# Six local re-orderings in a two-block transformer kernel: lead-in, softmax ends, feed-forward start, retention, recurrence, last norm

## The chip, the core and the metric

The kernel runs on one core of a Trainium2 chip. The metric is the device time of one execution in microseconds (us); the table further down gives the median of three runs. The engines run side by side and meet at semaphores: TensorE (PE) does the matrix products, VectorE (DVE) and ScalarE (ACT) the work on elements, GpSimd (POOL) a few additions, and SyncE (SP) issues the DMAs that bring the weights.

## The reference

Two blocks follow each other on a sequence of 256 rows of 1024 values. The first has two layers of three parallel attention branches and a gated feed-forward part with a convolution; the second has four layers (retention, a linear recurrence, latent attention, retention), each with a feed-forward part. Cut to what matters here:

```python
def first_block(x, ...):  # x: 1 x 256 x 1024, two layers
    for i in range(DEPTH):
        h = rms_norm(x, attn_norm[i])
        qa, ka, va, qb, kb, vb, qc, kc, vc, gates = jnp.split(h @ w_in[i], SPLIT_POINTS, axis=-1)
        ya = moba_attention(...)  # per head: rms_norm, rope, softmax(q k^T) v
        yb = sliding_window_sink_attention(...)
        yc = differential_attention(...)
        g = jax.nn.sigmoid(gates.reshape(B, S, N_BRANCH, D))
        merged = g[:, :, 0] * (ya @ w_pa[i]) + g[:, :, 1] * (yb @ w_pb[i]) + g[:, :, 2] * (yc @ w_pc[i])
        x = x + merged @ w_out[i]
        h = rms_norm(x, mlp_norm[i])
        u = causal_depthwise_conv(h @ w_up[i], conv_w[i], conv_b[i])   # 3 taps
        gate_u, val_u = jnp.split(u, 2, axis=-1)   # 2816 columns each
        x = x + (jax.nn.silu(gate_u) * val_u) @ w_down[i]
    return x

def second_block(x, ...):  # four layers: retention, rg-lru, mla, retention
    for i in range(DEPTH_2):
        mix = (retention_mixer, rglru_mixer, mla_mixer)[i % 3](h, ...)
        h = layer_norm(ALPHA * h + mix, ln_g[i, 0], ln_b[i, 0])
        h = layer_norm(ALPHA * h + square(relu(h @ w1[i])) @ w2[i], ln_g[i, 1], ln_b[i, 1])
    return h
```

All of it is computed in float32 from weights in HBM, some 375 MB in all, that are read once.

## The kernel before

**Tiling.** The sequence stands in two tiles of 128 rows (`tt` is 0 or 1). Each weight matrix is read in slots of 1 MB (128 x 2048 float32) into a ring of five buffers (`raw`, in the trace `slot`). To keep float32 accuracy, each slot is parted in a high and a low half: ACT copies it rounded to `slot_hi` (line 1460), DVE subtracts that from the slot into `slot_lo` (line 1955). The activations are parted in the same way (`split` tiles). A product is the sum of three: high x high, low weights x high, high weights x low, so a slot against both row tiles is 24 matmuls of 128 x 512 on PE.

**Rings and waits.** `slots` hands out the five buffers; SP waits for `slot_free` before it loads one. `banks` hands out the eight PSUM banks of 128 x 512 (`bank`; the upper four are also the accumulator `acc`); `banks.use(n, ...)` says how many are in use from there on and where the round starts. PE waits for `bank_read` before it fills a bank, the reading engine for `bank_full`. Each engine runs its own program in its own order, written out by hand; nothing passes an instruction that waits. `weights.ahead(u)` emits the splits of the slots up to three behind `u`, `weights.through(u)` those up to `u` itself.

**The stretches that the change touches.** Each engine has its own function of the same name.

- *Start.* ACT issues the two halves of `x`, SP the identity matrix, the gain table `tab`, and the slots of `w_in`. `rms_norm` squares (ACT 1495), takes the root (ACT 1497), scales (DVE 2012); PE turns the rows (`turned`, line 728) and ACT and DVE write the high and low parts (`hi_rows`, `lo_rows`). `head` on PE runs the first row tile over the first two slots, then the second. Behind the sixth slot SP issues twelve small loads `tokc` (line 592), and behind those the seventh slot.
- *Softmax ends.* `divisors(g)` on DVE (line 2186) scales the five groups of probabilities by their sums; PE turns them.
- *Feed-forward of the first block.* Eleven steps `s`, each with two slots of `w_up` (`gv` 0 is the gate half, 1 the value half). The products of step 0 come out of the head as rows and are turned back by PE (`turned_back`), and DVE copies them (line 2350); in the other steps each half has two sums `j` of one bank, which `summed(s, gv, j)` (line 2328) adds up. ACT scales (`scaled`), `convolved(s, gv)` on DVE (line 2338, four instructions) adds the other taps, ACT applies silu, POOL multiplies (line 2809), and ACT and DVE part the result (`hi_hidden`, `lo_hidden`). In layer 0 `angles(s - 1)` on DVE (lines 2060 to 2083) also computes, one piece a step, the rotation angles for the second block.
- *Retention.* Behind the four heads of group norm, `low(0)` to `low(7)` (line 2537) write the low parts of the turned gated rows; PE's next turning waits for the banks that `low` reads.
- *Recurrence.* `scans` (line 2642) run the recurrence on tiles of 128 channels, `gated` (2648) multiplies by the gate, `high_rows` on ACT (1828) and `low_rows` on DVE (2653) part the result. The groups are those of `LRU_ROWS`: 2, 4 and 4 tiles. `project("lwo", 5)` multiplies it by the five slots of `w_o`, slot c taking the tiles of channels in order.
- *End.* The last `layer_norm(7, True)` follows the last matmul: sum (DVE 2387), mean, squares (ACT 1698), root (ACT 1700), reciprocal, scale (DVE 2392, 2398), and four stores by SP.

## Time and profile before

| | us |
|---|---|
| median of 3 runs | 2083.84 |
| lowest, highest | 2083.83, 2084.2 |
| the profiled execution | 2085.47 |
| its span | 2083.7 |
| PE busy | 2050.8 (98%) |
| DVE busy | 1528.6 (73%) |
| ACT busy | 1052.6 (51%) |
| POOL busy | 158.7 (8%) |
| mean DMA rate | 181 GB/s |

The profiled execution took 1.63 us more than the median run, and 1.77 us of its time lie outside the span. Times in the rows count from the start of the span. A matmul's end is modelled, so neighbouring PE rows overlap a little; a stop of PE is best read from start to start, which makes it some 0.15 us longer than the idle time that the views give (at 1238.09 PE was idle for 1.45, but the matmul before started at 1236.25, and its kind follow each other by 0.23: 1.61). The granted clock (PEclk) is TensorE's clock in the stretch as a share of full speed: 1.00 stands for 2.4 GHz and 0.50 for 1.2 GHz.

### The profile page before, as it was taken

What the parts mean: (1) busy time and instruction counts of PE and PEld (TensorE: products, weight loads), DVE (VectorE), ACT (ScalarE), POOL (GpSimd) and SP (SyncE); (2) the same over time, 40 slices, a digit from 0 to 9 for tenths busy, and PEclk for the clock granted to TensorE, in tenths of its full rate; (3) what the DMA queues carried; (4) which work ended last, traced back from release to release, by engine and by line L of the source; (5) the groups of instructions that cost most, each with busy time, mean ns of one, the idle gap of its engine ahead of it and who ended that gap; (6) DMA issues with size and microseconds to landing.
All of it is one profiled execution on the core that took longest, in us unless ns stands there. A gap on an engine that the chain in (4) does not pass through costs nothing.

```text
span 2083.7 us, 27288 instructions
## 1 busy us (share of the span) xinstructions
PE 2050.8 (98%) x11335; PEld 1768.6 (85%) x11335; DVE 1528.6 (73%) x1677; ACT 1052.6 (51%) x1232; POOL 158.7 (8%) x94
## 2 busy tenths in 40 slices
PE   7999999999999999999999999999999999999998
PEld 6998888899978888878888988888888888778887
DVE  5878799787979777665766797666876667566665
ACT  4564555556556545454534575344653445455432
POOL 2001011030101204100000000000000005000000
PEclk9999999999999999999999999999999999999999
DMA  7544555564445555545655646654456556455662
GB/s 257 173 141 158 166 197 197 166 216 139 148 158 198 184 188 189 182 167 173 214 196 182 207 155 200 211 188 144 159 184 218 185 183 209 148 182 182 206 197 101
DMA packets 244724, 377.68 MB, mean 181 GB/s; under 512 B 14085, under 2 KB 179194, under 8 KB 244602
## 3 DMA queue, kind: packets, MB, share of 16 engines
q1 hardware_dynamic: 244314, 374.90, 54.6%
q8 instruction: 90, 1.47, 0.3%
q10 hardware_dynamic: 288, 1.05, 0.1%
q14 instruction: 32, 0.26, 0.0%
HBM read 374.87 MB, written 1.05 MB: 180 GB/s over the span
## 4 chain that ended last, share of the span: by engine, by line
PE 87%; DVE 6%; ACT 2%; DVEq 2%; DMA 1%; issue 0%; SPq 0%; ACTq 0%
PE bank L730 44%; PE acc L730 41%; DVE slot_lo L1955 3%; DVEq L1950 2%; PE bank L728 2%; ACT slot_hi L1460 1%; DMA slot<-in_w_in 1%; PE acc L728 0%; DVE arena L2029 0%; DVE arena L2186 0%; DVE arena L2642 0%; SPq L592 0%; DVE arena L2299 0%; DVE arena L2338 0%; ACT arena L1455 0%
## 5 line engine op out<-in xcount | busy, mean ns | idle before, releaser
L1955 DVE TENSOR_TENSOR slot_lo<-slot,slot_hi 128x2048 fp32r<-128x2048 f32 (+1 forms) x344 | 794.1, 2315 | 285.6 <-ACT slot_hi L1460 284.7
L1460 ACT ACTIVATE slot_hi<-slot 128x2048 fp32r<-128x2048 f32 (+1 forms) x344 | 652.1, 1904 | 386.7 <-DMA slot<-in_mlp_w 313.0
L730 PE MATMUL acc<-slot_hi,split 128*128 128x512 f32 (+1 forms) x2236 | 703.3, 389 | 2.9 <-DVE split L2653 1.5
L730 PE MATMUL bank<-split,slot_hi 128*128 128x512 f32 (+1 forms) x2524 | 575.3, 357 | 7.2 <-DVE arena L2328 6.9
L730 PEld LDWEIGHTS bank<-split,slot_hi 128*128 128x128 f32 x2524 | 439.6, 190 | 66.6 <-issue 8.6
L730 PEld LDWEIGHTS acc<-slot_hi,split 128*128 128x128 f32 x2236 | 418.1, 188 | 88.4 <-DVE split L2282 1.9
L730 PE MATMUL acc<-slot_lo,split 128*128 128x512 f32 (+1 forms) x1118 | 432.7, 387 | 0.0
L730 PE MATMUL bank<-split,slot_lo 128*128 128x256 f32 x2094 | 354.7, 283 | 0.0
L730 PEld LDWEIGHTS bank<-split,slot_lo 128*128 128x128 f32 x2094 | 310.7, 191 | 16.5
L730 PEld LDWEIGHTS acc<-slot_lo,split 128*128 128x128 f32 x1118 | 210.4, 188 | 39.7 <-issue 1.0
L730 PE MATMUL bank<-slot_hi,split 128*128 128x512 f32 (+1 forms) x804 | 227.7, 391 | 3.4 <-ACT split L1478 2.6
L730 PEld LDWEIGHTS bank<-slot_hi,split 128*128 128x128 f32 x804 | 150.3, 190 | 34.3 <-issue 4.6
L730 PE MATMUL bank<-slot_lo,split 128*128 128x512 f32 (+1 forms) x402 | 132.4, 388 | 0.0
L730 PE MATMUL acc<-split,slot_hi 128*128 128x256 f32 (+1 forms) x668 | 130.5, 305 | 0.0
L730 PEld LDWEIGHTS acc<-split,slot_hi 128*128 128x128 f32 x668 | 107.3, 191 | 5.7 <-issue 1.3
L1658 ACT ACTIVATE arena<-arena,par 128x256 f32<-128x256 f32 x88 | 48.1, 594 | 124.7 <-DVE arena L2328 117.6
L2411 DVE TENSOR_REDUCE arena<-bank 128x256 f32<-128x512 f32 x112 | 76.1, 687 | 42.9 <-PE bank L730 42.9
L1455 ACT ACTIVATE arena<-bank 128x512 f32<-128x512 f32 (+2 forms) x104 | 56.9, 569 | 91.2 <-PE bank L730 87.8
L2827 POOL TENSOR_TENSOR arena<-arena 128x512 f32<-128x512 f32 x16 | 28.0, 1753 | 955.7 <-ACT arena L1455 955.7
L730 PE MATMUL acc<-split,slot_lo 128*128 128x256 f32 x398 | 94.2, 283 | 0.0
L730 PEld LDWEIGHTS bank<-slot_lo,split 128*128 128x128 f32 x402 | 76.0, 189 | 16.0 <-issue 0.5
L2338 DVE SCALAR_TENSOR_TENSOR arena<-arena,par 128x254 f32<-128x254 f32 (+1 forms) x176 | 76.9, 479 | 3.6 <-issue 0.4
(230 smaller groups left out, 1476.0 us busy)
## 6 DMA issues: line engine op xcount, KB each, us to landing
slot<-in_mlp_w SPq DMA_DIRECT2D x128, 1024.0 KB, 5.3
slot<-in_ret_w_in SPq DMA_DIRECT2D x48, 1024.0 KB, 5.2
slot<-in_w_up SPq DMA_DIRECT2D x40, 1024.0 KB, 5.1
slot<-in_w_in SPq DMA_DIRECT2D x38, 1024.0 KB, 5.3
slot<-in_w_down SPq DMA_DIRECT2D x22, 1024.0 KB, 4.9
slot<-in_ret_w_o SPq DMA_DIRECT2D x16, 1024.0 KB, 4.8
slot<-in_lru_w_in SPq DMA_DIRECT2D x10, 1024.0 KB, 5.3
slot<-in_w_out SPq DMA_DIRECT2D x8, 1024.0 KB, 4.8
```

Of the source, the lines that this page charges most:

```text
L728: i = nc.tensor.transpose(o, w, ident)
L730: i = nc.tensor.matmul(o, w, m, start=start, stop=stop)
L1455: return A(o, i, func, **kw).then_inc(bank_read[u.r], 1)
L1460: A(whi[u.r][:, 0:u.cols], raw[u.r][:, 0:u.cols], ACT.Copy).then_inc(slot_hi[u.r], 1)
L1658: i = A(cgv[:, 2 * (s % 2) + j, gv, :], up_sums(s, gv, j), ACT.Identity, scale=par[:, L, PF_CW + 4 * FFT + f:PF_CW + 4 * FFT + f + 1], bia ...
L1950: dve.drain()
L1955: TTO(wlo[u.r][:, 0:u.cols], raw[u.r][:, 0:u.cols], f32(whi[u.r][:, 0:u.cols]), ALU.subtract)\
L2338: i = STT(out=y, in0=up_sums(s, gv, j)[:, 0:S - sh], scalar=par[:, L, PF_CW + (2 - sh) * 2 * FFT + f:PF_CW + (2 - sh) * 2 * FFT + f + 1], ...
L2411: RED(hq[:, s % NHID, j, :], bank[u.r][:, :].rearrange("p (i s) -> p s i", i=2), AX, ALU.add)\
L2827: TTO(rin[c % 2], rsum[c % 2][:, :, 0:S], rsum[c % 2][:, :, S:2 * S], ALU.add).then_inc(V["rot_summed"], 1)
```

## The change

Nothing of what is computed changes, and no load or split of weights is added or left out, except that the first slot's come in halves.

1. *Start.* `x[1]` is loaded by SP behind the first slot instead of by ACT at once. The first slot is loaded by two DMAs of 512 KB with a semaphore of their own for the first, and its high and low parts are made by halves (`first_norm` on ACT and DVE). The large `consts` load goes behind the fourth slot instead of the second. PE does twelve turnings of the identity into an unused bank before the first real one, and `first_head` runs both row tiles over the first slot, then both over the second. The projections that follow start at bank 4.
2. *Softmax ends.* `divisors(4)` stands ahead of the split of the first `w_p` slot.
3. *Feed-forward start.* ACT copies step 0's banks instead of DVE, scales step 0 at once, and its splits stand between; DVE's first three steps are written out with each `summed` ahead of a convolution. In the later steps ACT's `hi_hidden` goes from behind `scaled(s, 0)` to behind the next split, ahead of `scaled(s, 1)`. In layer 0 the angles start at step 3 (`angles(s - 3)`), and steps 9 and 10 take two pieces.
4. *Retention.* `low(0)` and `low(1)` stand in the step of the last head, ahead of a split.
5. *Recurrence.* The last four tiles go in two groups of two, with `gated(3)`, `high_rows(3)` and `low_rows(3)`.
6. *Last norm.* For the second row tile the last matmuls end by column halves, DVE takes mean and variance from `bn_stats` and `bn_aggr`, and ACT does the root alone.

```diff
-LRU_ROWS = (slice(0, 2), slice(2, 6), slice(6, 10))
+LRU_ROWS = (slice(0, 2), slice(2, 6), slice(6, 8), slice(8, 10))
...
-banks.use(NBANK)
+banks.use(NBANK, None, NSUM)
...
+if L == 0 and i == 0:
+    u = slots[f"w_in{L}", c]
+    sp.wait_ge(slot_free[u.r], u.uses + 1)
+    dst, src = what[0](u.r)
+    sp.dma_start(dst[:, 0:2, :], src[:, 0:2, :]).then_inc(V["first_loaded"], 16)
+    sp.dma_start(dst[:, 2:4, :], src[:, 2:4, :]).then_inc(slot_full[u.r], 16)
+    sp.dma_start(x[:, 1, :], I["x"][0, P:2 * P, :]).then_inc(V["x_loaded1"], 16)
+    continue
 put(slots[f"w_in{L}", c], *what)
-if i == 1 and L == 0:
+if i == 3 and L == 0:
     sp.dma_start(con[:, P:C_ALL], I["consts"][:, P:C_ALL]).then_inc(V["loaded"], 16)
 if i == 12:
...
+def first_rows_high(u, o, name):
+    w = [part[u.r][:, :].rearrange("p (k n) -> p k n", n=512) for part in (whi, wlo)]
+    h = hT[0][:, 0:4, 0:P]
+    pe.wait_ge(V["hi_out"], his[name, (0, 0)].uses + 1)
+    for a, halves in enumerate(((V["first_hi"], slot_hi[u.r]), (V["first_lo"], slot_lo[u.r]))):
+        for b in range(2):
+            pe.wait_ge(halves[b], 1)
+            for k in (2 * b, 2 * b + 1):
+                mm(o[:, :], h[:, k, :], w[a][:, k, :], (a, k) == (0, 0), False)
...
+def first_head(name, turned, us, bs):
+    for _ in range(12):
+        mm(bank[NBANK - 1][:, 0:P], ident, None, transpose=True)
+    turned(0)
+    opened = [open_bank(bs[0])]
+    first_rows_high(us[0], opened[0][0], name)
+    rows_low(us[0], opened[0][0], name, 0, 0, None)
+    turned(1)
+    opened.append(open_bank(bs[1]))
+    rows_high(us[0], opened[1][0], name, 1, 0)
+    rows_low(us[0], opened[1][0], name, 1, 0, None)
+    freed(us[0])
+    for tt in range(TT):
+        rows_high(us[1], opened[tt][0], name, tt, 1)
+        rows_low(us[1], opened[tt][0], name, tt, 1, opened[tt][1])
+    freed(us[1])
...
+    acc_halves(u, lhs[i], tt)
+    continue
 acc_rows(u, lhs[i], tt, False, last, V["acc_full"] if last else slot_free[u.r] if tt else None,
...
-project("lwo", 5, lru_rows, lambda c: pe.wait_ge(V["lru_y"], (1, 2, 2, 3, 3)[c]), ln_turned(2))
+project("lwo", 5, lru_rows, lambda c: pe.wait_ge(V["lru_y"], (1, 2, 2, 3, 4)[c]), ln_turned(2))
...
+squared(0)
+rooted(0)
+act.wait_ge(V["first_loaded"], 16)
+A(whi[r][:, 0:SLOT // 2], raw[r][:, 0:SLOT // 2], ACT.Copy).then_inc(V["first_hi"], 1)
+hi_rows(name, 0, [0])
+act.wait_ge(slot_full[r], 16)
+A(whi[r][:, SLOT // 2:SLOT], raw[r][:, SLOT // 2:SLOT], ACT.Copy).then_inc(slot_hi[r], 1)
+weights.next = 1
+squared(1)
+hi_rows(name, 0, [1])
+rooted(1)
+hi_rows(name, 1)
...
+back_copies(f"uph{L}", [0])
+weights.ahead(slots[f"up{L}", (0, 0)])
+back_copies(f"uph{L}", [1], 1)
+weights.ahead(slots[f"up{L}", (0, 1)])
+for gv in range(2):
+    u = banks[f"up{L}", (0, gv)]
+    full(act, u)
+    copy(cu[:, gv, :], bank[u.r][:, :], u)
...
-for s in range(11):
+for gv in range(2):
+    scaled(0, gv)
+weights.ahead(slots[f"up{L}", (1, 0)])
+silu(0, L * 11)
+for s in range(1, 11):
     n = L * 11 + s
     for gv in range(2):
         weights.ahead(slots[f"up{L}", (s, gv)])
+        if gv:
+            hi_hidden(s - 1, n - 1)
         scaled(s, gv)
-        if s and gv == 0:
-            hi_hidden(s - 1, n - 1)
     silu(s, n)
...
 high_rows(2)
+high_rows(3)
...
+def first_norm(name):
+    r = slots.made[0].r
+    scaled_rows(0, 0)
+    for c0, hi, lo in ((0, V["first_hi"], V["first_lo"]), (SLOT // 2, slot_hi[r], slot_lo[r])):
+        c = slice(c0, c0 + SLOT // 2)
+        dve.wait_ge(hi, 1)
+        TTO(wlo[r][:, c], raw[r][:, c], f32(whi[r][:, c]), ALU.subtract).then_inc(lo, 1)
+    weights.next = 1
+    lo_rows(name, 0, [0])
+    scaled_rows(0, 1)
+    lo_rows(name, 0, [1])
+    lo_rows(name, 1, [0])
+    weights.upto(1)
+    lo_rows(name, 1, [1])
...
 scores(4)
 divisors(3)
 y_low(2)
+divisors(4)
 weights.through(slots[f"w_p{L}", 0])
-divisors(4)
 weights.through(slots[f"w_p{L}", 1])
...
 summed(1, 0, 0)
-for gv in range(2):
-    u = banks[f"up{L}", (0, gv)]
-    full(dve, u)
-    T(cu[:, gv, :], bank[u.r][:, :]).then_inc(bank_read[u.r], 1)
 weights.ahead(slots[f"up{L}", (0, 1)])
-for gv in range(2):
-    convolved(0, gv)
-for s in range(1, 11):
+summed(1, 0, 1)
+convolved(0, 0)
+summed(1, 1, 0)
+convolved(0, 1)
+weights.ahead(slots[f"up{L}", (1, 0)])
+summed(1, 1, 1)
+summed(2, 0, 0)
+weights.ahead(slots[f"up{L}", (1, 1)])
+summed(2, 0, 1)
+convolved(1, 0)
+lo_hidden(his[f"hidb{L}", 0], 0)
+summed(2, 1, 0)
+convolved(1, 1)
+weights.ahead(slots[f"up{L}", (2, 0)])
+summed(2, 1, 1)
+weights.ahead(slots[f"up{L}", (2, 1)])
+for s in range(2, 11):
     for gv in range(2):
-        for j in range(2):
-            if (s, gv, j) != (1, 0, 0):
+        if s > 2:
+            for j in range(2):
                 summed(s, gv, j)
-        weights.ahead(slots[f"up{L}", (s, gv)])
+            weights.ahead(slots[f"up{L}", (s, gv)])
         convolved(s, gv)
         if gv == 0:
             lo_hidden(his[f"hidb{L}", s - 1], (s - 1) % NHID)
     if s > 2:
         weights.ahead(slots[f"down{L}", s - 2])
-    if L == 0:
-        angles(s - 1)
+    if L == 0 and s > 2:
+        angles(s - 3)
+        if s > 8:
+            angles(s - 1)
...
+def last_rows(n):
+    cs = [slice(h * 512, (h + 1) * 512) for h in range(HALVES)]
+    for h, c in enumerate(cs):
+        dve.wait_ge(V["acc_full"], 8 + 2 * n + 2 + h)
+        STT(out=xn[:, 1, c], in0=x[:, 1, c], scalar=ALPHA, in1=acc[:, 1, c], op0=ALU.mult, op1=ALU.add)
+        d()
+        nc.vector.bn_stats(col(BN + 6 * h, 6), xn[:, 1, c])
+    d()
+    nc.vector.bn_aggr(col(MV, 2), col(BN, 12))
+    d()
+    TS(col(LVAR), col(MV + 1), LN_EPS, None, ALU.add).then_inc(V["ln_mean"], 1)
+    for h, c in enumerate(cs):
+        STT(out=x[:, 1, c], in0=xn[:, 1, c], scalar=col(MV), in1=tab[:, c], op0=ALU.subtract, op1=ALU.mult)
+        if h == 0:
+            dve.wait_ge(V["ln_std"], 2 * n + 2)
+            nc.vector.reciprocal(col(LR + 1), col(LSTD + 1))
+        d()
+        STT(out=x[:, 1, c], in0=x[:, 1, c], scalar=col(LR + 1), in1=tab[:, D + h * 512:D + (h + 1) * 512],
+            op0=ALU.mult, op1=ALU.add).then_inc(V["out_ready"], 1)
...
     for tt, u in enumerate(us):
         TS(ro[:, tt, h * RDV:(h + 1) * RDV], bank[u.r][:, :], col(MV + 2 * tt), col(LR + tt),
            ALU.subtract, ALU.mult).then_inc(bank_read[u.r], 1)
+    if h == 3:
+        for i in range(2):
+            low(i)
     weights.ahead(slots[k + "w", 17 + 2 * h])
     if h:
         gated(h - 1)
-for i in range(2):
-    low(i)
 gated(3)
...
-scans(range(6, 10))
-for c in (8, 9):
-    evacuated(dve, banks["lw", c])
+scans((6, 7))
+evacuated(dve, banks["lw", 8])
 gated(2)
+scans((8, 9))
+low_rows(2)
 weights.ahead(slots["lwo", 0])
-low_rows(2)
+evacuated(dve, banks["lw", 9])
+gated(3)
+low_rows(3)
...
```

**The start on ACT.** The rows behind the first root, before: the whole first slot (`slot_49`), both halves of the first turned rows, the second slot, then the squares of `x[1]`.

```order
L1460 ACTIVATE slot_hi<-slot_49 128x2048 [waits slot_full0]
L1478 ACTIVATE split<-bank 128x4x128 [waits bank_full0]
L1478 ACTIVATE split<-bank 128x4x128 [waits bank_full1]
L1460 ACTIVATE slot_hi<-slot_50 128x2048 [waits slot_full1]
L1495 ACTIVATE xn,stat<-x 128x1024 [waits x_loaded1]
L1497 ACTIVATE stat<-stat 128x1 [waits var_ready]
L1478 ACTIVATE split<-bank 128x4x128 [waits bank_full3]
```

And now:

```order
L1559 ACTIVATE slot_hi<-slot_49 128x1024 [waits first_loaded]
L1524 ACTIVATE split<-bank 128x4x128 [waits bank_full0]
L1562 ACTIVATE slot_hi<-slot_49 128x1024 [waits slot_full0]
L1549 ACTIVATE xn,stat<-x 128x1024 [waits x_loaded1]
L1524 ACTIVATE split<-bank 128x4x128 [waits bank_full1]
L1553 ACTIVATE stat<-stat 128x1 [waits var_ready]
L1524 ACTIVATE split<-bank 128x4x128 [waits bank_full3]
L1524 ACTIVATE split<-bank 128x4x128 [waits bank_full0]
L1507 ACTIVATE slot_hi<-slot_50 128x2048 [waits slot_full1]
```

The second slot's copy moved behind all four `hi_rows`, and the squares of `x[1]` now stand between the two first ones.

**The feed-forward start on DVE**, layer 0, from `summed(1, 0, 0)` on, before (`slot_50` to `slot_53` and `slot_49` are the ring's buffers; 2328 is `summed`, 2350 the copy of step 0, 2338 `convolved`):

```order
L2328 TENSOR_REDUCE arena<-bank 128x256 [waits bank_full0]
L2350 COPY arena<-bank 128x512 [waits bank_full3]
L2350 COPY arena<-bank 128x512 [waits bank_full2]
L1955 TENSOR_TENSOR slot_lo<-slot_52,slot_hi 128x2048 [waits slot_hi3]
L2338 SCALAR_TENSOR_TENSOR arena<-arena,par 128x255 [waits conv_scaled]
L2338 SCALAR_TENSOR_TENSOR arena<-arena,par 128x255
L2338 SCALAR_TENSOR_TENSOR arena<-arena,par 128x254 x2
L2338 SCALAR_TENSOR_TENSOR arena<-arena,par 128x255 [waits conv_scaled]
L2338 SCALAR_TENSOR_TENSOR arena<-arena,par 128x255
L2338 SCALAR_TENSOR_TENSOR arena<-arena,par 128x254 x2
L2328 TENSOR_REDUCE arena<-bank 128x256 [waits bank_full1]
```

And now (2426 is `summed`, 2436 `convolved`):

```order
L2426 TENSOR_REDUCE arena<-bank 128x256 [waits bank_full0]
L2036 TENSOR_TENSOR slot_lo<-slot_52,slot_hi 128x2048 [waits slot_hi3]
L2426 TENSOR_REDUCE arena<-bank 128x256 [waits bank_full1]
L2436 SCALAR_TENSOR_TENSOR arena<-arena,par 128x255 [waits conv_scaled]
L2436 SCALAR_TENSOR_TENSOR arena<-arena,par 128x255
L2436 SCALAR_TENSOR_TENSOR arena<-arena,par 128x254 x2
L2426 TENSOR_REDUCE arena<-bank 128x256 [waits bank_full3]
L2436 SCALAR_TENSOR_TENSOR arena<-arena,par 128x255 [waits conv_scaled]
```

`summed(1, 0, 1)`, the row on `bank_full1`, stood behind two copies, a split and eight convolution rows; now one split stands between it and the sum ahead of it.

**The end of the recurrence on DVE**, before (`slot_50` holds the fourth slot of `w_o`, `slot_51` the fifth):

```order
L1955 TENSOR_TENSOR slot_lo<-slot_49,slot_hi 128x2048 [waits slot_hi0]
L2642 SCALAR_TENSOR_TENSOR arena<-arena 128x256 x4
L2648 TENSOR_TENSOR arena<-arena 128x1024 [waits bank_read3,bank_read2]
L1955 TENSOR_TENSOR slot_lo<-slot_50,slot_hi 128x2048 [waits slot_hi1]
L2653 TENSOR_TENSOR split<-arena,split 128x1024 [waits hi_out]
L1955 TENSOR_TENSOR slot_lo<-slot_51,slot_hi 128x2048 [waits slot_hi2]
L1955 TENSOR_TENSOR slot_lo<-slot_52,slot_hi 128x2048 [waits slot_hi3]
```

And now:

```order
L2036 TENSOR_TENSOR slot_lo<-slot_49,slot_hi 128x2048 [waits slot_hi0]
L2776 SCALAR_TENSOR_TENSOR arena<-arena 128x256 x2
L2782 TENSOR_TENSOR arena<-arena 128x512 [waits bank_read2]
L2776 SCALAR_TENSOR_TENSOR arena<-arena 128x256 x2
L2787 TENSOR_TENSOR split<-arena,split 128x512 [waits hi_out]
L2036 TENSOR_TENSOR slot_lo<-slot_50,slot_hi 128x2048 [waits slot_hi1]
L2782 TENSOR_TENSOR arena<-arena 128x512 [waits bank_read3]
L2787 TENSOR_TENSOR split<-arena,split 128x512 [waits hi_out]
L2036 TENSOR_TENSOR slot_lo<-slot_51,slot_hi 128x2048 [waits slot_hi2]
L2036 TENSOR_TENSOR slot_lo<-slot_52,slot_hi 128x2048 [waits slot_hi3]
```

The scans, the gating and the low part went from one row group to two, and the second group's two rows stand between the two last splits of the projection.

**The same place on ACT**, before (1828 is `high_rows`) and now (1908 is `high_rows`):

```order
L1828 ACTIVATE split<-arena 128x1024 [waits lru_product]
L1460 ACTIVATE slot_hi<-slot_49 128x2048 [waits slot_full0]
L1460 ACTIVATE slot_hi<-slot_50 128x2048 [waits slot_full1]
L1828 ACTIVATE split<-arena 128x1024 [waits lru_product]
L1460 ACTIVATE slot_hi<-slot_51 128x2048 [waits slot_full2]
L1460 ACTIVATE slot_hi<-slot_52 128x2048 [waits slot_full3]
```

```order
L1908 ACTIVATE split<-arena 128x1024 [waits lru_product]
L1507 ACTIVATE slot_hi<-slot_49 128x2048 [waits slot_full0]
L1507 ACTIVATE slot_hi<-slot_50 128x2048 [waits slot_full1]
L1908 ACTIVATE split<-arena 128x512 [waits lru_product] x2
L1507 ACTIVATE slot_hi<-slot_51 128x2048 [waits slot_full2]
L1507 ACTIVATE slot_hi<-slot_52 128x2048 [waits slot_full3]
```

The copy of `slot_51` stood behind one `high_rows`; now it stands behind two.

## Rows read from the trace of the kernel before

**Rows 1.** Who PE waited for, whole run: idle us, times, longest.

```profile
PE bank L730 <- DVE arena L2328: 6.9, 2, 3.4
PE bank L728 <- DVEq L2540: 1.5, 4, 0.4
```

**Rows 2.** Timeline, PE at the start: start, us, instruction, count, [idle before <-releaser].

```profile
13.16 2.04 PE L730 MATMUL bank<-slot_hi,split 128*128 128x512 f32 x4 [2.57 <-ACT split L1478]
...
24.02 1.98 PE L730 MATMUL bank<-slot_hi,split 128*128 128x512 f32 x8
...
28.59 0.47 PE L730 MATMUL bank<-slot_hi,split 128*128 128x512 f32 x1 [0.79 <-issue]
```

**Rows 3.** Timeline, ACT at the start.

```profile
10.62 1.91 ACT L1460 ACTIVATE slot_hi<-slot 128x2048 fp32r<-128x2048 f32 x1 [4.46 <-DMA slot<-in_w_in]
```

**Rows 4.** Timeline, DVE at the start.

```profile
7.56 0.16 DVE L2008 RECIPROCAL stat<-stat 128x1 f32<-128x1 f32 x1 [1.64 <-DMA tab<-in_attn_norm]
```

**Rows 5.** Busy by stretch: PE, PEld, DVE, ACT, POOL, PEclk, DMA share, GB/s.

```profile
235.18:240.44 5.26, 5.26 (x17) 4.49 (x17) 5.18 (x7) 3.36 (x4) 0.65 (x1) 0.50 0.59 199
...
615.68:620.06 4.38, 4.38 (x16) 3.66 (x17) 4.30 (x5) 3.37 (x4) 0.66 (x1) 0.61 0.62 201
...
13.00:18.20 5.20, 5.04 (x12) 3.78 (x13) 5.20 (x5) 3.33 (x5) 0.00 (x0) 1.00 1.04 390
```

**Rows 6.** DMA issues by line: count, KB each, median us to landing.

```profile
slot<-in_w_up SPq DMA_DIRECT2D x40, 1024.0 KB, 5.1
...
slot<-in_w_up SPq DMA_DIRECT2D x8, 512.0 KB, 4.9
```

**Rows 7.** The chain that ended last, 0 to 95 us: start, us, what.

```profile
25.34 0.38 SPq L523
...
31.54 11.90 DMA slot<-in_w_in
```

**Rows 8.** Timeline, PE at four later stops.

```profile
85.01 1.09 PE L728 MATMUL bank<-con,arena 128*128 128x128 f32 x8 [0.47 <-DVE arena L2143]
...
157.37 0.87 PE L728 MATMUL bank<-con,arena 128*128 128x128 f32 x6 [0.57 <-DVE arena L2186]
...
195.81 0.50 PE L730 MATMUL acc<-slot_hi,split 128*128 128x512 f32 x1 [0.51 <-DVE split L2282]
...
1238.09 0.50 PE L730 MATMUL acc<-slot_hi,split 128*128 128x512 f32 x1 [1.45 <-DVE split L2653]
```

**Rows 9.** Timeline, DVE in the first feed-forward steps.

```profile
230.87 3.56 DVE L2338 SCALAR_TENSOR_TENSOR arena<-arena,par 128x255 f32<-128x255 f32 x8
```

**Rows 10.** Timeline, DVE with the angles and at the feed-forward's end, layer 0.

```profile
350.38 2.13 DVE L2076 SCALAR_TENSOR_TENSOR arena<-trig,arena 128x1024 f32<-128x1024 f32 x1
...
370.94 0.69 DVE L2328 TENSOR_REDUCE arena<-bank 128x256 f32<-128x512 f32 x1 [2.00 <-PE bank L730]
...
385.79 0.69 DVE L2050 TENSOR_TENSOR split<-arena,split 128x512 fp32r<-128x512 f32 x1 [0.70 <-ACT split L1671]
```

**Rows 11.** POOL's product of the feed-forward, whole run: ns min/median/max.

```profile
L2809 POOL TENSOR_TENSOR arena<-arena x20: 1268/3218/3228, 234.6 to 744.5; 128x512 f32<-128x512 f32 x20
```

**Rows 12.** Timeline, a split on DVE beside POOL's additions.

```profile
174.15 3.42 DVE L1955 TENSOR_TENSOR slot_lo<-slot,slot_hi 128x2048 fp32r<-128x2048 f32 x1
```

**Rows 13.** Timeline, DVE in the retention, then at the recurrence's end.

```profile
923.91 2.29 DVE L1955 TENSOR_TENSOR slot_lo<-slot,slot_hi 128x2048 fp32r<-128x2048 f32 x1 [1.49 <-ACT slot_hi L1460]
...
1234.62 2.28 DVE L1955 TENSOR_TENSOR slot_lo<-slot,slot_hi 128x2048 fp32r<-128x2048 f32 x1
1236.82 1.22 DVE L2653 TENSOR_TENSOR split<-arena,split 128x1024 fp32r<-128x1024 f32 x1
1237.95 4.49 DVE L1955 TENSOR_TENSOR slot_lo<-slot,slot_hi 128x2048 fp32r<-128x2048 f32 x2
```

**Rows 14.** Timeline, ACT at the recurrence's end.

```profile
1235.70 5.76 ACT L1460 ACTIVATE slot_hi<-slot 128x2048 fp32r<-128x2048 f32 x3
```

**Rows 15.** Timeline, DVE at the end.

```profile
2076.04 1.22 DVE L2387 SCALAR_TENSOR_TENSOR xn<-x,acc 128x1024 f32<-128x1024 f32 x1 [3.29 <-PE acc L730]
```

102 lines of the change are left out of this document (57 added, 45 removed).

## The prediction

> **What bounds the kernel now.** I read the shares of busy time first: TensorE is busy for 98% of the span, so only its stops can be won, and the stretch in which its clock is low. The second view is the list of waits of PE. Of it two lines matter: 6.9 us in two stops behind `summed` and 1.5 us in four stops behind `low` [rows 1]. The timeline of PE gives the single stops: the first matmul of a weight at 13.16, one short stop at 28.59 [rows 2], then 85.01, 157.37, 195.81 and 1238.09 [rows 8]. For each stop I went to the engine named at its end and read what stands ahead of the awaited instruction there; where that chain is back to back, taking one link out of PE's own wait wins nothing. Last I read the stretches with their granted clock, since a stop can cost more than itself: behind the first feed-forward stop the clock is at 0.50 for 5.26 us, in layer 1 at 0.61 for 4.38 us, where it is near 1 elsewhere [rows 5].
>
> **1. Start.** The first slot is ready for PE 13.16 because it landed at about 10.6 and its high part took 1.91 more [rows 2, 3]. The DMA share is 1.04 there, at 390 GB/s [rows 5], so bytes decide. `x`, identity, gain table and first slot are about 2.6 MB, landed by 10.6. Counting back at 0.37 MB a us (my estimate between that row's 0.39 and the somewhat lower rate of the beginning): without `x[1]` ahead of it the table lands near 6.2 instead of 7.5 [rows 4], half the slot at 7.7, the other at 9.1, `x[1]` at 10.6. First half's high part to 8.7, first matmul near 9.5, 3.6 earlier. This lead isn't kept whole. `x[1]`'s squares, its scaling and the `hi_rows` put its turned rows on ACT until about 16.6, and only behind them stands the high part of the second slot, 18.5, and DVE's low part, 20.8. PE has done both tiles of the first slot at about 18.9, starts the second, stands for about 1 us for the low part, and has 20 matmuls of 0.227 us (eight take 1.98, the last 0.39 of it being pipeline [rows 2]) left: 25.4 where it is 27.65 now (sixteen from 24.02 on), 2.3 earlier. The stop at 28.59 (0.9 from start to start) came from a bank that now is another one, and goes: 3.2. At 85.01 a stop of 0.6 waits for DVE [rows 8]. That chain begins with the seventh slot, issued at 31.54, 6.2 behind the sixth at 25.34, and landing 11.9 later [rows 7]. The sixth slot's buffer now is free at about 18.9, the seventh's at 25.4, so it can be issued 6.1 earlier; if it only lands earlier by as much as the bytes ahead of it, the gain is 3.2. PE could gain 3.2 + 0.6. I take **-3.4**, bounds -2 and -5.
>
> The rows show two loads of 512 KB landing in 4.9 us where 1024 KB take 5.1 [rows 6]: on a queue with room, halving a load wins almost nothing. The Trainium skill ("DMA: Bandwidth & Descriptors", Anatomy of one DMA and Rules for kernel authors) goes the same way against this part: about 2.0 us fixed for each DMA plus bytes at 436 GB/s, at least 1 MiB for each, and spreading over issuing engines gives no bandwidth. By it half a slot alone would take an estimated 3.2 us and the whole 4.4, so the halving would win 1.2, and the move of `x[1]` to another queue only its place behind the slot; the start's gain would be some -2.5 instead of -3.4, and the sum 0.9 later.
>
> **2. Softmax ends.** The stops at 157.37 and 195.81 are 0.7 each. The first waits for `divisors(4)`, behind a split; that goes. The second waits for a low part at the end of a row of splits, sums and low parts on DVE that has hardly a gap from 161 on. The moved split is done no earlier than now, since `divisors(4)` itself waits for exponentials till nearly that time, so the row begins no earlier and what is won at the first stop is added at the second. **0** for both layers, bounds -1.5 (both stops of both layers half gone) and +0.4.
>
> **3. Feed-forward start, layer 0.** The stop is 3.4 idle [rows 1], 3.6 from start to start; the 5.26 us at clock 0.50 lose 2.6 [rows 5]. `summed(1, 0, 1)` stood behind eight convolution rows of 3.56 us [rows 9], two copies and a split that waited for ACT; it now stands behind one split. The order on DVE has slack of some 2.8 us to PE's demand by my count, ACT's copies are needed later than they are done, so both parts go: -6.2. Then the angles. Moving them back by two steps puts one more piece of 2.13 us [rows 10] into step 9 and one into step 10. At step 9 DVE idles 2.0 before 370.94 [rows 10] and hides it. In step 10 DVE has no gap: the last hidden low part, at 385.79 to 386.5 [rows 10], comes 2.2 to 2.5 later, at about 388.8, where PE asks for it near 387.3: a stop of 1.6; the rest of the lag goes on to the next norm, 0.5. Together +2.1. **-4.1**, bounds -6.2 (the tail is hidden) and -3.
>
> **4. Feed-forward start, layer 1.** No angles. 3.6 and 39% of 4.38, 1.7 [rows 1, 5]: **-5.3**, bounds -5.5 and -3.6 (the clock falls for another reason).
>
> **5. Retention.** Two stops a time, 1.5 idle in four, 0.15 more each from start to start: 2.1. `low(0)` and `low(1)`, 1.9 us together, go to where DVE has just been idle for 1.49 [rows 13], so nothing late follows but 0.4. **-2.1**, bounds -2.1 and -1.
>
> **6. Recurrence.** PE stops 1.6 at 1238.09 [rows 8]. Fourth slot's low part: from 1234.62, done at 1236.9 [rows 13]; the last low rows of all four tiles at 1238.0. By pairs, the first pair's rows are ready ahead of that split, so the fourth slot's product starts at 1237.0: 1.1 earlier. But the fifth slot's high part, on ACT, now stands behind `high_rows(3)`, which waits for `gated(3)`, which on DVE stands behind the split of the fourth slot: 1236.9 + 0.65 = 1237.6, `high_rows(3)` to 1238.2, the high part (5.76 / 3 = 1.92 [rows 14]) to 1240.1, DVE's low part (4.49 / 2 = 2.24 [rows 13]) to 1242.4. Now it is done at 1240.2, and PE wants it at 1238.09 + 12 x 0.227 = 1240.8. So **+1.6**, and PE stands for 2.7 in one piece (1239.7 to 1242.4). The trace has no stop of that length in this place: one of 1.45 is not followed by a low clock, two of 3.4 are [rows 1, 5, 8]. 2.7 is nearer to 3.4, so I add 1.6, about the smaller of the two losses (1.7): **+3.2**, bounds -1.6 (the stop just goes) and +4.2.
>
> **7. Last norm.** From 2076.04 DVE adds, means, scales till 2081.2 [rows 15]. By halves the first half's sum and statistics lie beside the last six matmuls; behind the last one stand one sum of 0.7, one `bn_stats` of 0.65, the aggregate 0.25 and four waits on DVE's own results, where 1.22, a mean and 1.15 of squares on ACT stood. The first store leaves 0.7 earlier, the second hardly. **-0.2**, bounds -1 and +0.2.
>
> Sum: -3.4 + 0 - 4.1 - 5.3 - 2.1 + 3.2 - 0.2 = -11.9. On the profiled execution's 2085.5 that is 2073.6, with its 1.6 above the median taken off **2071.9**.
>
> **Rivals.** *(a) No low clock behind the recurrence's stop*, as behind 1.45: 2070.3. For it: the stop is short of 3.4. *(b) The orders pay as meant*: the softmax stops go for good (-1.5) and the fifth slot is in time because the scans of a pair are done earlier than I count (-1.1 instead of +3.2): 2071.9 - 1.5 - 4.3 = 2066.1. Against it is the row order on ACT. *(c) The start gives -2 and the retention -1*, DVE's chain to 85 being bound by landings: 2074.4. *(d) The feed-forward starts only shift their stop*, because ACT, with four copies more ahead of its scaling, is late for the first `convolved`: half of 11.5 stays, 2077.6. *(e) Slower*: in the feed-forward of layer 0 DVE becomes the bound of every step. Its step is four sums of 0.65, three splits of 2.24, 3.56 of convolution and a low part of 0.65, 13.5 us [rows 9, 10, 13], 15.6 with angles, beside PE's three slots or 72 x 0.227 = 16.4. POOL's product takes 3.22 us in most steps where 1.27 is its lowest [rows 11], and a split beside POOL's additions took 3.42 instead of 2.28 [rows 12]; if the new order lets the product lie beside three splits, DVE's step is 15.6 + 3 x 1.14 = 19.0, 2.6 over PE's, times 8 steps is 21, of which the tail's 2.1 is part: 2090.8. It decides from 0.8 us more a step on; only half of a step's splits can meet one product, which speaks against it.
>
> **How the numbers follow.** Forecast 0.42, (a) 0.22, (b) 0.15, (c) 0.15, (d) 0.03, (e) 0.03. The likeliest time is 2071.9. From 2065.5, (b) and its bound, to 2075.5, (c) and its bound, lie all but (d), (e) and tails of the unknown prices: 0.8 or a little more. A measurement of this kernel tells about 0.2%, 4.2 us, from no change; below 2079.7 is faster. That holds for all but (e) and part of (d): faster 0.95, the same 0.02, slower 0.03.
>
> **What would show it.** Right: first matmul near 9.5, PE at the place of 28.59 about 3 us earlier; no stop at the second and third feed-forward steps and clock 1 there in both layers; a new stop of about 1.6 at the tail of layer 0's feed-forward behind `lo_hidden`, none in layer 1; the stop of 157 gone and that of 195.8 larger; no stops behind `low`; at the recurrence two stops, the second of 2 to 3 us behind the fifth slot's low part, and a clock below 1 behind it. Wrong: DVE without a gap through layer 0's steps; the start gaining less than 2 at 85; a fifth slot copied by ACT before 1240.

## The result, and the profile after

The changed kernel takes 2069.5 us (median of four runs, 2068.26 to 2070.33) where the kernel before takes 2083.84: 14.3 us or 0.7% less, ratio 0.9927 with a 95% interval of 0.9915 to 0.9939. Timed again on another chip it gave 0.9927 once more (0.9915 to 0.9939). The forecast was 2071.9 with a range of 2065.5 to 2075.5. The profiled execution took 2070.33 us with a span of 2067.7, 16.0 less than the span before; the medians differ by 1.7 less. Half of that is time outside the span, 2.6 us now and 1.8 before, and half is that the profiled execution of before lay 1.6 above its median and this one 0.8.

The waits of PE, changed kernel (who waited for whom, total, times, longest), answer [rows 1]. `summed` (2426 now) and `low` are gone from it, and the longest wait behind a split is the new one in the recurrence; the first row is the wait for the identity before the twelve turnings:

```profile
PE acc L736 <- DMA con<-in_consts: 4.1, 1, 4.1
PE acc L738 <- DVE slot_lo L2036: 3.0, 2, 2.6
PE acc L738 <- DVE split L2380: 0.8, 2, 0.4
```

PE's timeline at the start answers [rows 2]. The first weights are multiplied from 9.73 instead of 13.16, PE stands for the second slot's low part at 20.20, and the stop at 28.59 has no counterpart: `acc` banks are filled from 24.90 on, without one.

```profile
9.73 2.12 PE L738 MATMUL bank<-slot_hi,split 128*128 128x512 f32 x4 [0.21 <-ACT split L1524]
...
20.20 1.21 PE L738 MATMUL bank<-slot_lo,split 128*128 128x512 f32 x4 [0.66 <-DVE slot_lo L2036]
...
24.90 0.39 PE L738 MATMUL acc<-slot_hi,split 128*128 128x512 f32 x1
```

The later stops that are left, from PE's timeline, answer [rows 8]: the one behind the softmax (it has a like one in layer 1, at 565.10), a new one at the tail of layer 0's feed-forward, and two at the recurrence.

```profile
190.55 0.50 PE L738 MATMUL acc<-slot_hi,split 128*128 128x512 f32 x1 [0.41 <-DVE split L2380]
...
376.44 0.50 PE L738 MATMUL acc<-slot_hi,split 128*128 128x512 f32 x1 [0.45 <-DVE split L2146]
...
1219.50 0.47 PE L738 MATMUL acc<-slot_hi,split 128*128 128x512 f32 x1 [0.47 <-DVE slot_lo L2036]
...
1225.08 0.77 PE L738 MATMUL acc<-slot_hi,split 128*128 128x512 f32 x1 [2.58 <-DVE slot_lo L2036]
```

The stretches with their clock (columns as in [rows 5]): the feed-forward's first steps now run at 1.00 in both layers, where [rows 5] have 0.50 and 0.61, and the stretch behind the recurrence's long stop has 0.67.

```profile
1225.08:1230.20 5.12, 5.12 (x16) 4.14 (x17) 4.70 (x3) 2.61 (x3) 0.00 (x0) 0.67 0.01 3
226.29:231.50 5.21, 5.21 (x31) 4.54 (x30) 4.85 (x4) 2.57 (x4) 3.19 (x1) 1.00 0.59 201
600.88:606.00 5.12, 5.12 (x31) 4.45 (x30) 4.77 (x4) 2.58 (x4) 3.19 (x1) 1.00 0.63 205
```

Both programs issue the same matmuls behind the head, so each can be laid beside itself. The lead is how much earlier the changed kernel starts the same matmul; where it changes, a part has its price (a minus sign is a loss):

| place (time before) | lead, us | the part's gain | forecast |
|---|---|---|---|
| head's end, 28.59 | 3.7 | | 3.2 |
| 85.01 | 4.4 | start 4.4 | 3.4 |
| behind 195.81 | 5.3 | softmax, layer 0: 0.9 | 0 |
| 242 | 11.4 | first steps, layer 0: 6.1 | 6.2 |
| 400 | 10.4 | its tail: -1.0 | -2.1 |
| behind 576.35 | 11.2 | softmax, layer 1: 0.8 | 0 |
| 625 | 16.4 | first steps, layer 1: 5.2 | 5.3 |
| behind 929.59 | 17.5 | retention 1.1 | 1.05 |
| 1238.09, fourth slot | 18.6 | 1.1 | 1.1 |
| 1240.99, fifth slot | 15.9 | -2.7 | -2.7 |
| 1245 | 14.2 | clock: -1.7 | -1.6 |
| behind 1850.52 | 15.4 | retention and small shifts 1.2 | 1.05 |
| last store landed | 16.0 | norm and small shifts 0.6 | 0.2 |

### The profile page after: what moved, and what is told of

It is laid out like the page before. It is cut to its first block, busy times and chain, and to the rows that moved or that the text cites. A ratio compares the mean times of both kernels' runs of the same rounds, so it can differ in the third digit from the quotient of the medians.

```text
span 2067.7 us, 27322 instructions
## 1 busy us (share of the span) xinstructions
PE 2049.2 (99%) x11347; PEld 1768.4 (86%) x11347; DVE 1525.6 (74%) x1680; ACT 1052.9 (51%) x1236; POOL 168.1 (8%) x94
## 3 DMA queue, kind: packets, MB, share of 16 engines
HBM read 374.87 MB, written 1.05 MB: 182 GB/s over the span
## 4 chain that ended last, share of the span: by engine, by line
PE 94%; DVE 3%; ACT 1%; DVEq 1%; DMA 0%; issue 0%; SPq 0%
PE bank L738 48%; PE acc L738 44%; PE bank L736 2%; DVE slot_lo L2036 1%; DVEq L2031 1%; ACT slot_hi L1507 1%; PE acc L736 0%; DMA slot<-in_w_in 0%; DVE arena L2776 0%; DVE arena L2782 0%; DVE arena L2397 0%; ACT split L1524 0%; DVE arena L2350 0%; DVE arena L2436 0%; ACT arena L1502 0%
## 5 line engine op out<-in xcount | busy, mean ns | idle before, releaser
L738 PE MATMUL acc<-slot_hi,split 128*128 128x512 f32 x2236 | 713.1, 392 | 4.7 <-DVE slot_lo L2036 3.0
L738 PE MATMUL acc<-slot_lo,split 128*128 128x512 f32 x1118 | 436.7, 391 | 0.0
L738 PE MATMUL bank<-slot_hi,split 128*128 128x512 f32 (+1 forms) x804 | 219.0, 381 | 0.6 <-ACT split L1524 0.6
L2964 POOL TENSOR_TENSOR arena<-arena 128x512 f32<-128x512 f32 x16 | 27.9, 1745 | 958.1 <-ACT arena L1502 958.1
L2946 POOL TENSOR_TENSOR arena<-arena 128x512 f32<-128x512 f32 x20 | 60.6, 3028 | 298.0 <-DVE arena L2436 298.0
```

Of the source, the lines that this page charges most:

```text
L738: i = nc.tensor.matmul(o, w, m, start=start, stop=stop)
L2946: TTO(hq[:, s % NHID, :, :], sgl[:, 2 * (s % 2):2 * (s % 2) + 2, :], cgv[:, 2 * (s % 2):2 * (s % 2) + 2, 1, :], ALU.mult).then_inc(V["prod ...
L2964: TTO(rin[c % 2], rsum[c % 2][:, :, 0:S], rsum[c % 2][:, :, S:2 * S], ALU.add).then_inc(V["rot_summed"], 1)
```

## Experiments

All are the changed kernel with one thing different, and are compared with it by the places at which PE stops and by their leads; a single time scatters by more than most parts are worth. On the chip of the first four, before took 2084.34 us, on that of the next four 2084.89, on the last 2085.32.

**The recurrence in one group.** The edit takes part 5 of the change back, cut to its core:

```diff
-LRU_ROWS = (slice(0, 2), slice(2, 6), slice(6, 8), slice(8, 10))
+LRU_ROWS = (slice(0, 2), slice(2, 6), slice(6, 10))
...
 high_rows(2)
-high_rows(3)
```

> The changed kernel with the recurrence's last four tiles in one group again, all else as changed. Theory: the pairs cost 3.2 us in all (1.0 won at the fourth slot, 2.7 lost at the fifth, 1.6 by the clock at 0.67 of the stretch behind it), so this is about 3 us faster than the changed kernel: 2066.3, one stop of 1.6 near 1219.5, none at the fifth slot, clock 1.00 behind it. Rival: the fifth slot was late for a cause outside this part (its landing, say), so that the stop of 2.7 stays and the fourth slot's grows by 1: 2070.5.

2066.73 us. PE stops once:

```profile
1220.45 0.50 PE L738 MATMUL acc<-slot_hi,split 128*128 128x512 f32 x1 [1.46 <-DVE split L2786]
```

It is 0.95 later than the changed kernel at the fourth slot and 3.4 ahead behind the fifth. The pairs cost what the forecast said, and the rival is out.

**The fifth slot's parts first.**

```diff
 high_rows(2)
+weights.ahead(slots["lwo", 1])
 high_rows(3)
...
 gated(3)
+weights.ahead(slots["lwo", 1])
 low_rows(3)
```

> The changed kernel, with ACT's high part of the fifth slot of w_o ahead of high_rows(3), and DVE's low part of it ahead of low_rows(3). Theory: the fifth slot waited only for its place on ACT; DVE now works without a gap (split of slot 4 to 1219.35, gated(3) to 1220.0, split of slot 5 to 1222.3, low_rows(3) to 1222.95), stops of 0.6 at both slots, the clock stays at 1.00: 2.1 + 1.6 = 3.7 faster than the changed kernel, 2065.8, and 0.5 faster than with one group. Rival: the buffer or the landing of slot 5 is the limit: the stop of 2.7 stays, 2069.5.

2066.29 us. DVE's timeline, and PE's two stops:

```profile
1219.40 0.69 DVE L2783 TENSOR_TENSOR arena<-arena 128x512 f32<-128x512 f32 x1
1220.01 2.28 DVE L2037 TENSOR_TENSOR slot_lo<-slot,slot_hi 128x2048 fp32r<-128x2048 f32 x1
1222.21 0.69 DVE L2788 TENSOR_TENSOR split<-arena,split 128x512 fp32r<-128x512 f32 x1
```

```profile
1219.45 0.47 PE L738 MATMUL acc<-slot_hi,split 128*128 128x512 f32 x1 [0.48 <-DVE slot_lo L2037]
...
1222.95 0.50 PE L738 MATMUL acc<-slot_hi,split 128*128 128x512 f32 x1 [0.51 <-DVE split L2788]
```

DVE runs without a gap and the fifth slot is multiplied from 1222.95, the time worked out. So the place of the fifth slot's two parts was the whole of the long stop; ACT's copy and DVE's split were moved together, and no run moves one alone. What is left, two stops of 0.6, is DVE's own work. Over one group the pairs in this order win 0.2 us at this place of the trace, not 0.5: less than the executions of one kernel scatter. (The trace with one group has one more stop that the others lack, 0.7 at 1455; it isn't part of this.)

**The start as before.** The hunks on the loads, on `first_head`, on both `first_norm` and on `banks.use` taken back.

> The changed kernel with the whole start as before (both x loads by ACT, whole first slot, old head, consts behind the second slot, banks from 0). Theory: the start is worth the lead of 4.4 us that the traces show at the stop of 85.0, and nothing behind depends on it: 2073.9, first matmul of a weight at 13.2, and the softmax gains of 0.8 a layer stay. Rival: the softmax gain of layer 0 came from the earlier DMAs of the start: then 5.2 are lost, 2074.7, and the stop of 0.7 at the fifth divisors is back in layer 0.

2074.58 us, and the stop of before is back:

```profile
84.79 0.87 PE L728 MATMUL bank<-con,arena 128*128 128x128 f32 x6 [0.69 <-DVE arena L2198]
```

4.2 us are lost at that place, and both new divisors' places stay free of a stop: the rival is out. In layer 1 the second stop behind the softmax is 0.4 longer than in the changed kernel (0.78 idle at 569.74), so the two parts are nearly, not quite, independent.

**The angle pieces early.**

```diff
-if L == 0 and s > 2:
-    angles(s - 3)
-    if s > 8:
-        angles(s - 1)
+if L == 0:
+    for a in {3: (0, 1), 4: (2, 3), 5: (4,)}.get(s, (s - 1,) if s > 5 else ()):
+        angles(a)
```

> The changed kernel with the angle pieces 0 to 4 put in steps 3 to 5 and pieces 5 to 9 in steps 6 to 10, one a step as before the change. Theory: the stop of 0.6 at the tail of layer 0's feed-forward comes from piece 7 (1.23 us) in step 10; with it gone the kernel is 0.6 to 0.9 faster than the changed one, 2068.8. Rival: DVE has no room in steps 3 to 5 either and the lag appears there: a stop at step 4 or 5 of 1 to 2 us, 2070.5.

2067.5 us. The tail's stop is gone, and no other stop came. The lead over the changed kernel, 0.3 us from the start, is 1.3 behind the tail: the pieces' place was worth 1.0.

**The softmax order back.**

```diff
-divisors(4)
 weights.through(slots[f"w_p{L}", 0])
+divisors(4)
```

> The changed kernel with divisors(4) behind the split of the first w_p slot again in both layers. Theory (from the two traces): the order itself is worth 0.7 a layer, since the stop behind it did not grow: 1.5 us slower than the changed kernel, stops of 0.7 near 152 and 523. Rival, the forecast's: DVE's row to the next stop is what counts; the new stops are there, but those near 190 and 565 shrink from 0.6 by as much: no difference.

2071.46 us. The stops are there, and those behind them, start to start, have grown from 0.57 to 0.67 and from 0.58 to 0.70 instead of shrinking:

```profile
152.90 0.76 PE L736 MATMUL acc<-con,arena 128*128 128x128 f32 x5 [0.71 <-DVE arena L2284]
...
191.34 0.50 PE L738 MATMUL acc<-slot_hi,split 128*128 128x512 f32 x1 [0.51 <-DVE split L2380]
```

1.7 us are lost from start to start, 0.9 in layer 0 and 0.8 in layer 1. The forecast's zero is wrong, and DVE's timeline shows why. The split behind the merged heads starts at 156.85 here and at 156.82 in the changed kernel: up to there the row on DVE is no later with the old order, as the forecast had it. Twelve us on, one split takes 3.43, where the changed kernel's takes 2.42. Old order, then new:

```profile
169.68 3.43 DVE L2036 TENSOR_TENSOR slot_lo<-slot,slot_hi 128x2048 fp32r<-128x2048 f32 x1
```

```profile
169.41 2.42 DVE L2036 TENSOR_TENSOR slot_lo<-slot,slot_hi 128x2048 fp32r<-128x2048 f32 x1
```

That is [rows 12], 3.42 too. POOL's additions run beside it, and what DVE wins, POOL loses, and more. POOL's timeline, old order, then new:

```profile
168.41 2.56 POOL L2939 TENSOR_TENSOR arena<-arena 128x512 f32<-128x512 f32 x2 [115.67 <-DVE arena L2350]
```

```profile
168.38 5.85 POOL L2939 TENSOR_TENSOR arena<-arena 128x512 f32<-128x512 f32 x3 [115.84 <-DVE arena L2350]
```

The second addition takes 1.30 with the old order and 3.34 with the new. Which one is held up goes by which one starts first. In the twelve traces with the new order the split starts 0.21 to 0.24 ahead of POOL's second addition, in both layers, and takes 2.41 to 2.43 while the addition takes 3.34 to 3.37. In the two with the old order, before and this run, it starts 0.01 to 0.02 behind, in both layers, and takes 3.42 to 3.44 while the addition keeps its 1.30. So with the new order DVE comes first, and PE waits for DVE's row. The order as such won the first stop; that the second didn't grow is the 1.0 us that DVE no longer waits for POOL. That last step is read from the traces; no run takes POOL's additions away.

**The first slot whole.**

```diff
-sp.dma_start(dst[:, 0:2, :], src[:, 0:2, :]).then_inc(V["first_loaded"], 16)
-sp.dma_start(dst[:, 2:4, :], src[:, 2:4, :]).then_inc(slot_full[u.r], 16)
+sp.dma_start(dst, src).then_inc(slot_full[u.r], 16)
```

with one high and one low part.

> The changed kernel with the first slot loaded by one DMA and parted whole; x[1] still behind it on SP. Theory: bytes decide, the whole slot lands at 9.4 where its first half lands at 8.1 and its second at 9.4, and its high part takes 1.9 instead of 1.05, so the first matmul of a weight starts near 12 instead of 9.7 and 1.5 to 2 of it are left at 80: about 1.7 us slower than the changed kernel. Rival, by the Trainium skill (DMA: Bandwidth & Descriptors, Rules for kernel authors: at least 1 MiB a DMA): the single load is the cheaper one, the slot lands before 9.4 and the kernel is no slower.

2073.48 us. The slot lands at 9.24, 1.2 us after the half did (8.07) and 0.2 before the second half (9.40), so the large load is in fact no slower a byte: the rival was right on the landing. But the whole copy stands ahead of everything:

```profile
9.26 1.91 ACT L1559 ACTIVATE slot_hi<-slot 128x2048 fp32r<-128x2048 f32 x1
```

```profile
11.31 2.04 PE L737 MATMUL bank<-slot_hi,split 128*128 128x512 f32 x4 [1.80 <-ACT slot_hi L1559]
```

PE is 1.6 later at the first matmul and 2.7 at the second tile, since the squares and rows of `x[1]` move behind the copy too, and 2.7 to 3.0 from there on. The halving is worth more than expected, and not by its loads: it lets ACT and DVE begin, and a rule on the size of a DMA doesn't see that.

**Without the twelve turnings.**

```diff
-for _ in range(12):
-    mm(bank[NBANK - 1][:, 0:P], ident, None, transpose=True)
```

> The changed kernel without PE's twelve turnings of the identity before the first rows. Theory: PE's clock is full earlier because it has been busy from 4.1 on; without them the matmuls from 9.7 on follow each other by 0.45 for about 1 us longer, PE is later at the second tile and the kernel 0.5 to 1.0 us slower. Rival: the turnings end before the wait for the rows and change nothing; same time, same place at which the distance of matmuls falls to 0.23.

2069.33 us. The first weights start at 9.61 and the head ends at the same time to 0.1; matmuls follow each other by 0.43 until about 13 in both. In this pair the turnings do nothing, as the rival had it. But the pair doesn't settle it. Of the eleven traces with the turnings seven have distances of 0.23 to 0.34 from the first weights on, where PE doesn't wait, and four have 0.43; the three without them (before, the start as before, this one) all have 0.43. Of the 0.8 that the seven have won by 13, the waits near 15 and 20 take most back, and the head ends 0.15 to 0.3 earlier (six of them; the seventh has another change there). So the turnings may be worth up to 0.3 in some executions; three traces without them are too few to show it. This execution has a stop of 0.6 at 81.8, and one of 0.7 at 47.2, that the changed kernel's first trace has not; the changed kernel run again stops at both places too (below), so they aren't the turnings'.

**The sums behind the convolution.**

```diff
-summed(1, 0, 1)
 convolved(0, 0)
-summed(1, 1, 0)
 convolved(0, 1)
+summed(1, 0, 1)
+summed(1, 1, 0)
```

> The changed kernel with one thing of the feed-forward's start as before: summed(1,0,1) and summed(1,1,0) on DVE stand behind both convolutions of step 0; ACT still copies step 0's banks. Theory: the stop came from the place of the sum on DVE: a stop of 2 to 3 us near 224 and 599, and perhaps the low clock behind it: 4 to 8 us slower than the changed kernel. Rival: taking the copies off DVE was enough: no stop over 0.5, no more than 1 us slower.

2069.33 us, and no stop near 224 or 600. The place of the sums, which the forecast named as the cause of its largest terms, doesn't bring the stop back alone. DVE does the split right behind the first sum:

```profile
217.53 0.69 DVE L2426 TENSOR_REDUCE arena<-bank 128x256 f32<-128x512 f32 x1 [2.09 <-PE bank L738]
218.14 2.28 DVE L2036 TENSOR_TENSOR slot_lo<-slot,slot_hi 128x2048 fp32r<-128x2048 f32 x1
220.34 3.56 DVE L2436 SCALAR_TENSOR_TENSOR arena<-arena,par 128x255 f32<-128x255 f32 x8
223.82 1.28 DVE L2426 TENSOR_REDUCE arena<-bank 128x256 f32<-128x512 f32 x2
```

Eight convolution rows take their 3.56 as in [rows 9], and the sum still comes in time.

**The changed kernel again.**

> The changed kernel once more, for the comparisons of this chip. 2069.5. The low clock behind the recurrence's stop of 2.7 was in the trace of the changed kernel (1.6 us), but not in two of four later traces that have the same stop; if chance decides, the single times scatter over about 1.6 us.

2070.19 us, 2068.18 to 2070.76. At 90 it is 0.8 behind its first trace, though the head ended 0.3 earlier: PE stops for 0.4 at 46.7 and for 0.6 at 81.3, each time for DVE:

```profile
81.32 1.09 PE L736 MATMUL acc<-con,arena 128*128 128x128 f32 x8 [0.43 <-DVE arena L2241]
```

The chain of it begins with the seventh slot, which was issued at 25.15 and landed 14.96 later, at 40.1. The traces with the first slot in halves agree: landings of 38.8 to 39.2 leave a stop of 0.1 at most, 39.3 to 39.6 one of 0.1 to 0.5, and 40.1 to 40.6 one of 0.6 and the one near 47 as well:

```profile
25.15 14.96 DMA slot<-in_w_in
```

The clock behind the recurrence's stop is 0.67 again.

**The copies on DVE.**

```diff
 weights.ahead(slots[f"up{L}", (0, 1)])
-for gv in range(2):
-    u = banks[f"up{L}", (0, gv)]
-    full(act, u)
-    copy(cu[:, gv, :], bank[u.r][:, :], u)
```

on ACT, and the loop of before behind `summed(1, 0, 0)` on DVE.

> The changed kernel with the copies of step 0's banks on DVE again, where they stood before the change, ACT's splits and DVE's sums at their new places. Putting the sums behind the convolutions alone brought no stop back, so the stop must come from the copies' engine or from ACT's order. Theory: it came from ACT's order (the high part of the next slot stood behind a scaling that waited for DVE's copies, and DVE was idle for 2.4 us before its split for it); with the splits ahead of the scaling no stop over 0.6 comes back: within 0.6 us of the changed kernel. Rival: DVE's 1.3 us of copies are too much at this place: a stop of 1 us or more near 223 and 598 and perhaps a low clock, 2 to 5 us slower.

2068.61 us, no stop in either layer. So neither the place of the sums nor the engine of the copies, taken alone, brings the stop back. What both runs without a stop share is ACT's order. In it the high parts of the two next slots stand between the copies of the turned rows:

```profile
210.85 1.93 ACT L1507 ACTIVATE slot_hi<-slot 128x2048 fp32r<-128x2048 f32 x1
214.43 0.60 ACT L1502 ACTIVATE arena<-bank 128x512 f32<-128x512 f32 x1 [1.65 <-PE bank L738]
214.92 1.91 ACT L1507 ACTIVATE slot_hi<-slot 128x2048 fp32r<-128x2048 f32 x1
218.52 2.08 ACT L1727 ACTIVATE arena<-arena,par 128x256 f32<-128x256 f32 x4 [1.69 <-DVE arena L2444]
```

Before the change ACT did the first of them only behind both copies, and the second behind a scaling that waited for DVE's copies; DVE's split of it then waited for ACT in turn (the idle 2.37 at 228.66):

```profile
220.25 1.91 ACT L1460 ACTIVATE slot_hi<-slot 128x2048 fp32r<-128x2048 f32 x1
225.72 1.10 ACT L1658 ACTIVATE arena<-arena,par 128x256 f32<-128x256 f32 x2 [3.56 <-DVE arena L2350]
226.72 1.90 ACT L1460 ACTIVATE slot_hi<-slot 128x2048 fp32r<-128x2048 f32 x1
```

```profile
228.66 2.29 DVE L1955 TENSOR_TENSOR slot_lo<-slot,slot_hi 128x2048 fp32r<-128x2048 f32 x1 [2.37 <-ACT slot_hi L1460]
```

The run with ACT's old order and the rest new, and the one with the sums and the copies both old, weren't made; that ACT's order alone is enough is therefore likely, not shown.

**Three mends together.** The two edits above (fifth slot first, angles early), and on ACT the second slot's high part ahead of the second tile's rows:

```diff
 rooted(1)
+weights.upto(1)
 hi_rows(name, 1)
```

> The changed kernel with three mends: the fifth slot's parts ahead of the second pair's (as in the run with the fifth copy first), the angle pieces early, and ACT's high part of the second slot of w_in ahead of hi_rows of the second tile. Theory: 3.7 (or 2.1 where the clock doesn't fall) and 1.2 as measured singly, and 0.7 from the second slot, whose low part then is ready at 18.8 instead of 20.1, with the second tile 0.4 later: 5 us under the changed kernel, 2064.5. Rival: the start's part is lost again (the second tile's rows stand behind the copy, and the stop only moves): 2065.2.

2065.9 us, 4.3 less than the changed kernel on the same chip; over before the ratio is 0.9907 (0.9892 to 0.9922), the best of all. The start's mend is worth nothing: at the head's end PE is 0.3 ahead of the changed kernel on this chip, but stops of 0.7 at 46.7 and 0.6 at 81.3 take it back, behind the same late landing, 40.1. The rival was right on that part.

**Retention and norm as before.** The hunks on `low` and on `last_rows` taken back.

> The changed kernel with the retention's low(0), low(1) and the whole last norm as before. The two lie far apart in the trace and are read singly. Theory: the four stops of 0.5 behind low are back, 2.1 in all (1.07 a time), and the end is 0.2 longer (from the start of the last matmul to the last store's landing 7.64 instead of 7.48): 2.3 us slower. Rival: at the new distance of the engines one of the retentions doesn't stop: 1.2 slower.

2071.61 us, on a trace with four stops of 0.52 to 0.55 behind `low`, two by two, 1.1 us lost each time. The norm is a miss: from the start of the last matmul (2062.55) to the landing of the last store (2069.82) it is 7.27 us here with the old form and 7.64 in the trace of before, where it is 7.48 with the new one in each of the changed kernel's two traces (of the ten others eight have 7.5 and two 7.9). The old form waits for a sum over 1024 and its own mean,

```profile
2062.98 1.22 DVE L2491 SCALAR_TENSOR_TENSOR xn<-x,acc 128x1024 f32<-128x1024 f32 x1 [3.29 <-PE acc L738]
...
2066.35 1.41 DVE L2502 SCALAR_TENSOR_TENSOR x<-x,stat,tab 128x512 f32<-128x512 f32 x2
```

and the new one begins its last scaling at 2064.50, 4.70 behind its last matmul's start (2059.80), and ends it 5.45 behind; the old ends at 5.21 here. So by halves nothing is won, and perhaps 0.2 lost.

## Why the prediction was right, and where it wasn't

**Recurrence**, the only term with the other sign, was right in all its steps: 1.0, -2.7 and the clock. ACT's order was read from the program, the times from the rows, and the run with the fifth copy first moved the stop to the hundredth worked out. What these traces can't forecast for one execution is the clock. Ten traces have the stop of 2.7; the same stretch of two of them, with the angles early and of the changed kernel again:

```profile
1223.78:1228.90 5.12, 5.12 (x23) 4.24 (x24) 5.12 (x3) 2.61 (x3) 0.00 (x0) 1.00 0.01 3
```

```profile
1225.86:1230.98 5.12, 5.12 (x16) 4.04 (x17) 4.69 (x3) 2.62 (x3) 0.00 (x0) 0.67 0.01 3
```

The low clock came in six of the ten and cost 1.5 to 1.6 us, and in none of the three changed traces without that stop. The forecast and rival (a) are one kernel in different executions; that the profiled one had the low clock was chance as far as these traces tell.

**Start**, -3.4 forecast, -4.4 or -3.7 by execution. The landings were right (half at 8.07 for 7.7, first matmul 9.73 for 9.5, head's end 24.9 for 25.4). PE's own lead, 3.7 at the head and the stop of 85 besides, was thought to be capped by DVE's chain at 3.2, since the seventh slot would land 3.2 earlier. The cap exists, but the landing moves by execution: 4.5 earlier in the first trace, where no stop is left, and 3.3 in the second, where the lead is 3.7. The estimate beside it, from the Trainium skill ("DMA: Bandwidth & Descriptors", Anatomy of one DMA), is by a cost that this section gives for DMAs issued by GpSimd, and SP issues these. The difference it gives, 1.2 between half a slot and the whole, is what the landings show (8.07 and 9.24); what the halving is worth to PE, 2.7 to 3.0, is not, since ACT's and DVE's rows behind it move too.

**Softmax**, 0 forecast, -1.7 measured. The reasoning that the first stop's gain would be given back at the second held as far as it went: DVE's row starts no earlier. The failed step is that the durations in that row stay. A split in it had a row of its own [rows 12], 3.42 us beside POOL, and I used it as a price for the slower rival only, not as 1.0 us that the row could win; it takes 2.42 now.

**Feed-forward starts**, right in size (6.1 and 5.2 for 6.2 and 5.3), not in cause. I named the rows between PE's stop and the awaited sum on DVE, among them a split that waited for ACT, and didn't follow that wait of 2.37 into ACT's order. Putting the sums back cost nothing, nor did putting the copies back. Since the change mended all three at once, the sum came out right, and the size was taken from the stop itself: this is luck as far as the cause goes.

**Tail of layer 0**, the term that was mis-sized: +2.1 forecast, +1.0 measured. The mechanism is right, as the run with the angles early shows; the price of a piece is not, and that is 0.9 of the 1.1. [rows 10] have it at 2.13 us, and in step 10 it took

```profile
372.21 1.23 DVE L2172 SCALAR_TENSOR_TENSOR arena<-trig,arena 128x1024 f32<-128x1024 f32 x1
```

**Retention** came as worked out. **The last norm** was forecast at -0.2; its traces give -0.2 and +0.2 by the old form's execution, which is no gain shown. The failed step is that ACT's squares were counted as time on the path. In the old form they lie beside DVE's first scaling,

```profile
2077.91 1.15 ACT L1698 ACTIVATE arena<-xn,stat 128x1024 f32<-128x1024 f32 x1 [6.85 <-DVE stat L2390]
```

```profile
2077.96 1.28 DVE L2392 SCALAR_TENSOR_TENSOR x<-xn,stat,tab 128x1024 f32<-128x1024 f32 x1
```

and DVE waits only 0.30 for the root behind them; the new form puts `bn_stats` and the aggregate, 0.69 and 0.21, on DVE instead.

**Of the rivals**, (b) was right on the softmax and wrong on the recurrence. (c) and (d) didn't come, nor did (e), DVE as the bound of a step, though its sign is there in part: in layer 0 DVE shows no idle time over 0.15 from 229.28 to 292.08. But PE doesn't stop in that stretch, and from 293.09 on DVE waits for PE once a step, 0.7 to 1.7.

Against the sum of -11.9 the span became 16.0 shorter: 1.0 of the difference is the start's, 1.7 the softmax's, 1.1 the tail's in layer 0, and 0.3 small shifts. The time outside the span is 2.6 in the profiled execution of after and 1.8 in that of before, and the medians lie 0.8 and 1.6 under the profiled times, which leaves 14.3 between the medians, 2.4 more than forecast.

## What to carry to other kernels

When a wait's chain leads to a feeding engine, follow that engine's own waits one engine further before naming what stands ahead, and price each instruction of the chain by whether another engine, here POOL, ran beside it and which of the two started first: the prices of the softmax and of layer 0's tail failed on that. When a group is cut in two to release its first half earlier, look at what is queued behind the second half on every engine that handles it; here a slot's copy behind the new small row cost nearly three times what the pairs won. Laying two traces side by side by their equal matmuls prices every part of a compound change at once.

## What the runs showed of the hardware that I hadn't expected

- The same `scalar_tensor_tensor` on 128 x 1024 takes 2.13 us where POOL's product runs (in five of five such pieces of before and after the two overlap, as 355.61 in the changed kernel beside a product from 353.44 to 356.66) and 1.23 where POOL is idle. I had taken the larger one as its price.

```profile
355.61 2.13 DVE L2172 SCALAR_TENSOR_TENSOR arena<-trig,arena 128x1024 f32<-128x1024 f32 x1
```

- DVE and POOL hold each other up, and the one that starts second pays: a split of 2.28 took 2.42 while POOL's addition, started 0.2 later, took 3.34 instead of 1.30; started 0.02 behind the addition, it took 3.43. The 3.22 us of POOL's product in [rows 11] are of this kind: a split started 0.22 ahead of it.

```profile
348.00 2.28 DVE L1955 TENSOR_TENSOR slot_lo<-slot,slot_hi 128x2048 fp32r<-128x2048 f32 x1
```

```profile
348.22 3.22 POOL L2809 TENSOR_TENSOR arena<-arena 128x512 f32<-128x512 f32 x1 [13.38 <-DVE arena L2338]
```

- A stop of PE of 2.7 us is followed by the lower clock in some executions of one and the same program and not in others; one of 3.4 idle, in two places of before, was followed by it both times, and one of 1.5 in neither of its two traces. A single profile can't price such a stop.
- The same load, the seventh slot, landed at 38.8 in one trace and at 40.6 in another, issued at 25.3 in both, and PE's stop at 81 comes and goes with it.
